# Split query and key factors and lag three in the second attention, with reordered loads and stores elsewhere

## The reference

```python
logits = jnp.einsum('bqmd,blmd->bmql', qb, k).astype(jnp.float32)
logits = logits + jnp.moveaxis(bias, -1, 0)[None]
logits = jnp.where((rel >= 0)[None, None], logits, -jnp.inf)
p = jax.nn.softmax(logits, axis=-1).reshape(bsz, B_HEADS, 2, BLOCK_Q, L)
a = p[:, :, 0] - lam * p[:, :, 1]
return jnp.einsum('bhql,blhe->bqhe', a.astype(v.dtype), v)
```

## Time and profile before

| | |
|---|---|
| median of 3 runs | 3950.34 us (3942.68 to 3954.74) |
| the profiled execution | 3951.39 us, span 3949.3 us, mean granted PE clock 0.937 |
| PE busy | 3468.5 us (88% of the span) |
| weight loads (PEld) | 2506.8 us, beside the matmuls |
| DVE busy | 2108.9 us (53%) |
| ACT busy | 2018.6 us (51%) |
| POOL busy | 534.6 us (14%) |
| the stages | front to 257, a_att 929 to 1830, b_qkgv 2110 to 2858, b_att 2858 to 3674, b_out from 3674 |

### The profile page before, as it was taken

One profiled execution on the slowest core, in us unless ns is written; L12 is line 12 of the kernel. 1 busy time (PEld: TensorE's weight loads), 2 busy tenths in 40 slices (PEclk: granted clock), 3 DMA queues, 4 the chain that ended last, 5 costly groups with the idle time before them and its releaser, 6 DMA issues. The chain is left out here.

```text
span 3949.3 us, 63256 instructions
## 1 busy us (share of the span) xinstructions
PE 3468.5 (88%) x18146; PEld 2506.8 (63%) x18146; DVE 2108.9 (53%) x5803; ACT 2018.6 (51%) x3487; POOL 534.6 (14%) x556
## 2 busy tenths in 40 slices
PE   5668798876999999996985999999988888889799
PEld 3546454455666666664864888889945555555687
DVE  3449799995555555554644000000077777777344
ACT  2438689963777777775224111111065666666222
POOL 2000155101111111110110111111030000000011
PEclk8889899986999999998997999999999999999898
DMA  6762477663322322323542222222231111110342
GB/s 209 158 161 43 152 227 230 188 207 94 85 82 77 81 78 81 81 82 127 162 138 88 76 70 74 75 69 67 65 99 41 46 46 46 46 46 27 116 141 97
DMA packets 399606, 402.71 MB, mean 102 GB/s; under 512 B 73376, under 2 KB 324672, under 8 KB 398656
## 3 DMA queue, kind: packets, MB, share of 16 engines
q1 hardware_dynamic: 390704, 400.49, 34.1%
q10 hardware_dynamic: 8720, 0.03, 0.1%
HBM read 254.66 MB, written 145.75 MB: 101 GB/s over the span
## 5 line engine op out<-in xcount | busy, mean ns | idle before, releaser
L1244 DVE CUSTOM_DVE_ANT_0 a_att_sb_lg<-a_att_ps_s,mask 128x512 f32<-128x512 f32 (+3 forms) x512 | 302.2, 595 | 236.4 <-PE a_att_ps_s L1138 196.8
L393 ACT ACTIVATE b_qkgv_sb_o_lo<-b_qkgv_ps_acc 128x512 f32<-128x512 f32 x128 | 76.6, 598 | 638.5 <-PE b_qkgv_ps_acc L376 473.3
L1275 DVE MEMSET b_att_sb_mx<- 128x256 f32 x1 | 0.3, 272 | 722.5 <-PEq L88 722.5
L1318 ACT ACTIVATE a_att_sb_pT<-a_att_ps_t 128x512 f32<-128x512 f32 (+3 forms) x640 | 315.7, 530 | 105.8 <-PE a_att_ps_t L1154 99.0
L1246 DVE TENSOR_SCALAR_CACHE_REDUCE b_att_sb_lg<-b_att_ps_s 128x512 f32<-128x512 f32 (+3 forms) x512 | 289.8, 591 | 137.1 <-PE b_att_ps_s L1143 126.9
L1310 ACT ACTIVATE b_att_sb_lg<-b_att_sb_lg,b_att_sb_negm 128x384 f32<-128x384 f32 (+15 forms) x256 | 305.7, 1198 | 111.0 <-DVE b_att_sb_negm L1252 110.5
L1310 ACT ACTIVATE a_att_sb_lg<-a_att_sb_lg,a_att_sb_negm 128x384 f32<-128x384 f32 (+15 forms) x256 | 307.3, 1201 | 78.0 <-DVE a_att_sb_negm L1252 78.0
L1154 PE MATMUL a_att_ps_t<-ident,a_att_sb_lg 128*128 128x128 f32 x2176 | 339.7, 279 | 0.0
L1143 PE MATMUL b_att_ps_s<-b_att_sb_k,b_att_sb_q 64*128 64x512 f32 (+3 forms) x1280 | 324.3, 593 | 14.1 <-DMA b_att_sb_k<-scratch_kT 9.8
L1137 PE MATMUL a_att_ps_s<-a_att_sb_k,a_att_sb_q 128*128 128x512 f32 (+3 forms) x640 | 287.2, 449 | 48.1 <-DMA a_att_sb_k<-scratch_kT 28.6
L1672 DVE TENSOR_SCALAR_CACHE_REDUCE mask<-scores,threshold_bits 128x384 bf16<-128x384 f32 (+8 forms) x288 | 322.6, 1187 | 1.2
(11 more groups left out here) (272 smaller groups left out, 6868.0 us busy)
## 6 DMA issues: line engine op xcount, KB each, us to landing
select_sb_w_gate<-in_a_w_in SPq DMA_DIRECT2D x32, 512.0 KB, 4.8
mask_sb_mod_w<-in_mod_w SPq DMA_DIRECT2D x16, 1024.0 KB, 6.5
a_att_sb_q<-scratch_qT SPq DMA_DIRECT2D x128, 128.0 KB
a_att_sb_q<-scratch_qT SPq DMA_DIRECT2D x256, 64.0 KB
a_att_sb_k<-scratch_kT SPq DMA_DIRECT2D x64, 256.0 KB
b_qkgv_sb_w<-in_b_w_in SPq DMA_DIRECT2D x32, 512.0 KB
front_sb_mod_w<-in_mod_w SPq DMA_DIRECT2D x8, 1024.0 KB, 6.8
scratch_hT<-front_sb_h SPq DMA_DIRECT2D x32, 256.0 KB, 3.6
```

Source lines behind the costliest of these rows:

```text
L1244: x = nc.vector.tensor_tensor_reduce(out, src, tab, 1.0, 2 * NEG, sign, ALU.max, top[:, col:col + 1])
L1318: nc.scalar.activation(pT[:, r % 2, a:z, c:c + P], t_ps[:, n % TR, 0:z - a], ACT.Copy).then_inc(t_left, 1)
```

## The change

Six things change, in both layers:

1. Front, SP: each slice of narrow weights is loaded right behind a modulation half; the last two follow x of group 1. The store of the bias goes to ACT's queue, behind the eight `leave_h` of group 0.
2. a_att: q part 0 and each piece of K are loaded as two DMAs of 64 rows, one for each part.
3. b_qkgv: the jobs of q and k become "split".
4. b_att: q and K hold a high and a low part, loaded apart; a chunk is three F32R terms for each map, six matmuls on 64 rows in place of two float32 ones. LAG is 3 for M = 2, so turns, leaves and values come a place later.
5. In both attentions `copy_near` stands ahead of the exponentials of the head's last place, with a wait for that place's maximum.
6. POOL splits five of the eight slices of b_att's output weights; b_out loads the other three itself behind `gp`, and splits them on ACT and DVE ahead of its first group.

```diff
@@ stage_front, SP and ACT
                 sp.wait_ge(mod_used, n - 1)
                 load_modulation(n)
+                if n >= 4:
+                    sp.wait_ge(w_lo_done, n - 3)
+                load_w(n - 2)
             load_x(1)
-            for k in range(KD):
-                if k >= 2:
-                    sp.wait_ge(w_lo_done, k - 1)
+            for k in range(KD - 2, KD):
+                sp.wait_ge(w_lo_done, k - 1)
                 load_w(k)
...
-                    if 4 * g + j == 2:
-                        sp.wait_ge(bias_done, 1)
-                        sp.dma_start(bias_dram, bvec[:].unsqueeze(1).to_broadcast([NMAPS, P, 384])).then_inc(bias_stored, 16)
...
             for k in range(KD):
                 leave_h(0, k)
+            act.wait_ge(bias_done, 1)
+            act.dma_start(bias_dram, bvec[:].unsqueeze(1).to_broadcast([NMAPS, P, 384])).then_inc(bias_stored, 16)
...
@@ stage_attention
+EARLY_OUT = 5
...
+    LAG = 2 if V2 else 3
...
-        q = st.sb("q", [P, QS, 2, PAIR], F32R) if V2 else st.sb("q", [P, QS, PAIR], F32)
-        k = st.sb("k", [P, 2, T], F32R if V2 else F32)
+        q = st.sb("q", [P, QS, 2, PAIR], F32R)
+        k = st.sb("k", [P, 2, T] if V2 else [P, 2, 2, T], F32R)
...
-                    sp.dma_start(q[:, r % QS, 0].bitcast(F32), q_dram[0:2, rows, cols]).then_inc(q_in[r % QS], 16)
                     for part in range(2):
+                        sp.dma_start(q[part * HD:(part + 1) * HD, r % QS, 0].bitcast(F32), q_dram[part, rows, cols]).then_inc(q_in[r % QS], 16)
                         sp.dma_start(q[(1 - part) * HD:(2 - part) * HD, r % QS, 1].bitcast(F32), q_dram[part, rows, cols]).then_inc(q_in[r % QS], 16)
                 else:
-                    sp.dma_start(q[:, r % QS], q_dram[0, ds(h * P, P), cols]).then_inc(q_in[r % QS], 16)
+                    for part in range(2):
+                        sp.dma_start(q[:, r % QS, part].bitcast(F32), q_dram[part, ds(h * P, P), cols]).then_inc(q_in[r % QS], 16)
...
-                dst = k[:, ds(h % 2, 1), keys].rearrange("p o t -> p (o t)")
                 if V2:
-                    sp.dma_start(dst.bitcast(F32), k_dram[0:2, ds(h * HD, HD), keys]).then_inc(k_in, 16)
+                    dst = k[:, ds(h % 2, 1), keys].rearrange("p o t -> p (o t)")
+                    for part in range(2):
+                        sp.dma_start(dst[part * HD:(part + 1) * HD].bitcast(F32), k_dram[part, ds(h * HD, HD), keys]).then_inc(k_in, 16)
                 else:
-                    sp.dma_start(dst, k_dram[0, ds(h * P, P), keys]).then_inc(k_in, 16)
+                    for part in range(2):
+                        dst = k[:, ds(h % 2, 1), part, keys].rearrange("p o t -> p (o t)")
+                        sp.dma_start(dst.bitcast(F32), k_dram[part, ds(h * P, P), keys]).then_inc(k_in, 16)
 
...
-                for c in range(KD):
+                for c in range(EARLY_OUT):
...
-                    for m in range(M):
-
-                        rows = slice(m * HD, (m + 1) * HD)
-                        nc.tensor.matmul(s_ps[:, (n + m) % SR, 0:z - a], q[rows, p // 2 % QS, cols], k[rows, slot, a:z],
-                                         start=True, stop=True).then_inc(s_done, 1)
+                    for j, (x, y) in enumerate(((0, 0), (1, 0), (0, 1))):
+                        for m in range(M):
+
+                            rows = slice(m * HD, (m + 1) * HD)
+                            mm = nc.tensor.matmul(s_ps[:, (n + m) % SR, 0:z - a], q[rows, p // 2 % QS, x, cols], k[rows, slot, y, a:z],
+                                                  start=(j == 0), stop=(j == 2))
+                            if j == 2:
+                                mm.then_inc(s_done, 1)
...
+                    if x == NB:
+
+                        act.wait_ge(near_in, head * 16 * M + 32 * M)
+                        act.wait_ge(max_done, head * NB + NB)
+                        copy_near(head)
                     if 1 <= x <= NB:
                         for m in range(M):
                             exps(head, x - 1, m)
-                    if x == NB:
-
-                        act.wait_ge(near_in, head * 16 * M + 32 * M)
-                        copy_near(head)
...
@@ stage_output, for b_out
-            for k in range(KD // 2 if split is None else 0):
-                sp.dma_start(w[:, k], weights[k * P:(k + 1) * P, :]).then_inc(w_in[k], 16)
+            for k in range(K0, KD // 2):
+                sp.dma_start(w[:, k - K0], weights[k * P:(k + 1) * P, :]).then_inc(w_in[k], 16)
...
-            for k in range(KD // 2, KD if split is None else KD // 2):
-                sp.dma_start(w[:, k], weights[k * P:(k + 1) * P, :]).then_inc(w_in[k], 16)
+            for k in range(max(K0, KD // 2), KD):
+                sp.dma_start(w[:, k - K0], weights[k * P:(k + 1) * P, :]).then_inc(w_in[k], 16)
...
-            for k in range(KD if split is None else 0):
+            for k in range(K0, KD):
                 after(act, w_in[k], 16)
-                nc.scalar.activation(w_hi[:, k], w[:, k], ACT.Copy).then_inc(w_hi_done, 1)
+                nc.scalar.activation(w_hi[k], w[:, k - K0], ACT.Copy).then_inc(w_hi_done, 1)
             after(act, consts_set, M)
...
@@ the calls
-            stage_project(nc, sems, "b_qkgv", [Job("whole", hT, KD, lambda n: win[:, :, ds(n * P, P)], KD, HD ** -0.5, qT[0]),
-                                               Job("whole", hT, KD, lambda n: win[:, :, ds(n * P + D, P)], KD, 1.0, kT[0]),
+            stage_project(nc, sems, "b_qkgv", [Job("split", hT, KD, lambda n: win[:, :, ds(n * P, P)], KD, HD ** -0.5, qT[0], qT[1]),
+                                               Job("split", hT, KD, lambda n: win[:, :, ds(n * P + D, P)], KD, 1.0, kT[0], kT[1]),
```

More of the change, by code:

```diff
@@ L1886, in stage_output @@
     with Stage(nc, sems, name) as st:
[L1887 to L1888 removed]
+        K0 = 0 if split is None else EARLY_OUT
+        w = st.sb("w", [P, KD - K0, D], F32)
+        late_hi, late_lo = (st.sb(n, [P, KD - K0, D], F32R) for n in ("w_hi", "w_lo"))
+        w_hi, w_lo = ([split[i][:, k] for k in range(K0)] + [late[:, k - K0] for k in range(K0, KD)] for i, late in ((0, late_hi), (1, late_lo)))
         gp = st.sb("gp", [P, D], F32)
```

24 lines of the change are left out of this document (10 added, 14 removed).

## The result

The changed kernel takes 3886.62 us (median of 4 runs, 3881.41 to 3890.77), the one before 3952.54 beside it: 0.9838 of it, with a 95% interval of 0.9827 to 0.9849. That is 66 us faster, where 78.5 were forecast. The profiled execution has a span of 3886.0 us, 63.3 less than before.

What follows compares the result with a forecast made beforehand. In b_att PE and DVE wait for each other in turn, neither alone filling it; other idle lies at starts. -31 - 19 + 0 + 3.5 - 45 + 1 + 12 = -78.5 from 3951.4: 3873 us, range 3838 to 3920.

Steps and rivals of the forecast that it cites:

- Front: -8 - 26.3 + 3.: Front: first projection 8 us earlier, PE's 26.3 us stall at the bias store gone, 3 charged for shared engines: -31.
- The rival that the bias takes the engines wherever it is issued: Front: stores of h land late on either queue, so only the 8 us are gained: 3896, chance 0.10.
- a_att's start -19, steady part 0.: a_att: wider K loads let PE start 19 us sooner, 7 us after K's first issue; added issues cost nothing later.
- b_qkgv 0.: b_qkgv: extra DVE passes and 16.8 MB more stores stay hidden under PE's 721 us: 0.
- b_att's start +3.5.: b_att's start: K is 2 MB in place of 1, and the second costs 3 to 5 us: +3.5.
- b_att, steady: -5.6 x 8 = -45: b_att: lag three and F32R save 5.6 us a head in places 2 to 9, 0 elsewhere; +1 to drain.
- The 51.5 for places 2 to 9.: b_att, head 6: places 2 to 9 fall from 57.1 to 51.5 us, bound by DVE's 48.02 us plus handing over.
- F32R takes from the second: b_att, places 2 to 9: F32R chunks of 0.85 us, from 1.06, cut DVE's 7.8 us wait for logits.
- b_out's start +12.: b_out's start: three late weight slices and their casts delay ACT's squares, so PE's head sums start 12 us later.
- `copy_near` 0.: Both attentions: the copy ahead of the exponentials moves 0.6 us before work DVE doesn't wait for: 0.
- The rival on the other side (halves one after the other): b_att chunks: F32R halves don't run side by side, 1.56 us a chunk, +52 in place of -45: 3970, chance 0.07.
- The rival of the wait that only changes its name: b_att: handing over through four shared banks limits DVE and PE, so only -13 us is gained: 3905, chance 0.14.

Runs made afterwards that it cites:

- e1: The kernel before with only the bias store moved to ACT's queue: 3937.19 us, ratio 0.9947.
- e2: The kernel before with only the six narrow weight slices loaded between the modulation halves: 3941.49 us, ratio 0.9971.
- e10: The changed kernel with casts behind squares in b_out, DVE's loop taking two heads a pass in b_att alone, bias store behind front block 12: 3884.04 us.
- e3: The kernel before with only a_att's K and q part 0 loaded as DMAs of 64 rows, one for each part: 3932.98 us, ratio 0.9952.
- e4: The kernel before with only LAG 3 in b_att, logits still float32: 3932.51 us, ratio 0.9944.
- e9: The changed kernel with DVE's loop over heads taking two heads in one pass, in both attentions: 3898.90 us, ratio 0.9852.
- e5: The changed kernel with LAG 2 again in b_att, logits still of three F32R terms: 3905.24 us, ratio 0.9879.
- e7: The changed kernel with ACT's three weight casts at b_out's start put behind the squares, ahead of the square root: 3874.47 us, ratio 0.9807.
- e12: The changed kernel with copy_near back behind the exponentials of a head's last place, without the wait for that place's maximum: 3887.51 us, ratio 0.9841.

## Why the prediction was right, and where its sizes were off

Direction and order of magnitude held, and so did the mechanism of every large term except F32R's part in b_att; the forecast of 3873 was 14 us low, inside its range. By its own terms:

- **"Front: -8 - 26.3 + 3."** -25.7, and 28 on the mean of the executions. The stall went (e1). The 8 for the first projection was right (8.6 in e2, about 8.7 over all). The charge of 3 for sharing engines was too small: e1 shows 26.3 - 18.5 = 8. The rival that the bias takes the engines wherever it is issued was right for that part, 8 of 26: ACT's queue freed SP's order, not the engines, and e10 shows the same store cost more at a later place.
- **"a_att's start -19, steady part 0."** -16.2 and -1.1; e3 alone -16.7 and -0.9. SP reached K 2.5 us after its first q issues, and PE began 8.4 behind it, not 7.
- **"b_qkgv 0."** PE's time from first to last was 709.3 and 709.6.
- **"b_att's start +3.5."** +6.0. At 0.7 us for each piece of 256 KB, four pieces more are 2.9, the low end of the 3 to 5 that I gave the second megabyte. The first piece also lands 0.9 us later behind its issue, and two others come 0.9 and 1.0 later than the rest of the row. The issue of K takes 5.42 us where it took 1.86, which I had not counted; whether it causes these delays is not shown.
- **"b_att, steady: -5.6 x 8 = -45", +1 to drain.** -36.3. Of the nearly 8 us that lack, 3.3 are in places 2 to 9 (-5.2 x 8 = -42), 2.5 in the rest, where lag three and F32R were to cancel and cost 0.4 a head, and 2.2 at the end (+3.2 for +1). That -5.2 comes near -5.6 is partly luck. "57.1 - 5.6 = 51.5" was read from head 6 alone, which went from 57.09 to 55.05, and 2.0 x 8 would have been -16. Over the eight heads the mean went from 58.7 to 53.5: the start was 1.6 us higher than I put it, because heads 0 to 4 had taken 58.5 to 62.0, and the end 2.0 us higher.
- **The 51.5 for places 2 to 9.** 53.5 on the mean. The lag removes the first wait as named (82.5 to 5.9 us in e4, 6.4 in the changed kernel). The floor of DVE was reached in places 3, 4 and 5, 8 and 9 of head 6, with 0.1 us idle in each, but not at place 6, where DVE's loop begins anew and stalls. The trace of before has the stall too, a place earlier, where a pass of the loop ended then: in head 6 DVE idles 2.00 us ahead of a chunk that PE had issued 4 us before, and the profile puts that down to PE. I had read it as a wait between engines that the change would lift. e9, which takes away four of six stalls, gives back 11 us. Behind PE's 5.39 us without work the granted clock is at its lower level, and it is 0.88 in places 2 to 9 of head 6, where it was 1.00.
- **"F32R takes from the second", with a chunk of 0.85.** A chunk is 0.90, and its worth is 13 to 14 us (e4, e5), but not where the prediction put it. In places 2 to 9, where DVE was said to wait for logits, F32R gives 0.3 to 0.4 us a head; nearly all its worth is in the places where PE bounds. So the 5.6 was for both parts, and what came of it is the lag's.
- **"b_out's start +12."** +9.9, by the sequence named; e7 takes it all back. (The steps added up to 3696.8 - 3686.2 = 10.6, not 10.7.)
- **`copy_near` 0.** e12: nothing.

The rival on the other side (halves one after the other) is excluded by the chunk of 0.90 us. The rival of the wait that only changes its name was partly true of the lag: in e4 52 of 77 us moved to DVE's banks, and in the changed kernel PE waits 64.0 us there where it waited 2.7, but 22 us were gained.

## What to carry to other kernels

When two engines hand work to each other, removing one wait is worth what is left between it and the next floor; price the second engine's own idle time first, stalls of its loop included, since moving the other engine's work does not lift those. Read such a price from several repeats of the loop: here one head of eight stood for all, and it gained less than half of the mean. A large store moved to another queue frees the order of the first queue, not the engines: look for what it will share them with, and which buffers wait for a landing. Put work that waits for a late load behind the work whose result another engine already waits for.

## What was not expected of the hardware

- A DVE loop body of one head in a_att ran without a stall; the body of two heads stalled 3.3 to 3.6 us at each of six jumps, with 47 fetch packets in place of 7, and the stage was 26 us longer.
- F32R matmuls on different 64-row halves ran side by side when the program had the three of one half first: starts in pairs 10 ns apart, 0.97 us for six, the last pair one of each half. The Trainium skill, "TensorE: Matmul & The Clock Gate", section "The mechanism", calls matmuls strictly first in, first out, which this order of starts does not agree with; the measurement decides here.
- A store read from one SBUF partition ran at 21 GB/s, one read from sixteen at 82 to 90 (38.4 and 34.9 us for 3072 KB).
